# Two low parts of each mixed token set move from VectorE to GpSimd, at the three places where products of seven begin

## The reference, cut to what matters

```python
b_g, c_g, v, z = jnp.split(h @ w_in, 4, axis=-1)     # convolution layer, in
...
return y @ w_out, padded[:, -(CONV_WIDTH - 1):]       # convolution layer, out
...
return (o * jax.nn.silu(z)) @ w_out                   # attention layer, out
```

## Time and profile before

| | value |
|---|---|
| three executions, median (us) | 2051.11 |
| the profiled execution, own time (us) | 2052.14 |
| its span in the trace (us) | 2050.5 |
| TensorE busy | 1978.3 us, 96% |
| TensorE weight load busy | 1865.1 us, 91% |
| VectorE busy | 1304.5 us, 64% |
| ScalarE busy | 805.1 us, 39% |
| GpSimd busy | 237.8 us, 12% |
| mean granted TensorE clock | 0.99 |

### The profile page before, as it was taken

How to read it: one execution, slowest core, us unless ns; L and a number is a source line. 1 busy time by engine, 2 the same in 40 slices (tenths; PEclk the granted TensorE clock), 3 DMA queues, 4 the chain that set the end, 5 groups by cost and what they waited for, 6 DMA issues and landing times.

```text
span 2050.5 us, 42506 instructions
## 1 busy us (share of the span) xinstructions
PE 1978.3 (96%) x16316; PEld 1865.1 (91%) x16316; DVE 1304.5 (64%) x1992; ACT 805.1 (39%) x1222; POOL 237.8 (12%) x155
## 2 busy tenths in 40 slices
PE   4989999999999999999999999999999999999995
PEld 3889999999999999999999999999888876679995
DVE  4677777777777777797778820223443446659777
ACT  3243333333333333455455532223453434435443
POOL 1200000000000000000000333333122122201002
PEclk9999999999999999999999999999999999999997
DMA  9966655555555556744464222335313249752447
GB/s 392 406 214 220 206 202 190 190 197 205 205 206 199 198 194 207 258 142 135 140 249 175 84 83 83 103 124 170 93 52 101 82 156 340 232 162 91 141 158 268
DMA packets 128276, 371.79 MB, mean 181 GB/s; under 512 B 13170, under 2 KB 39666, under 8 KB 125874
## 3 DMA queue, kind: packets, MB, share of 16 engines
q1 hardware_dynamic: 123058, 353.64, 49.4%
q0 software_dynamic: 5120, 16.78, 2.7%
HBM read 343.76 MB, written 26.61 MB: 181 GB/s over the span
## 4 chain that ended last, share of the span: by engine, by line
PE 87%; DVE 5%; DMA 4%; ACT 1%; issue 1%; SPq 1%; POOL 0%; DVEq 0%; ACTq 0%
PE ps L879 31%; PE ps L883 15%; PE ps L767 8%; PE ps L774 4%; PE ps L833 3%; DMA s<-adastream 3%; PE ps L1335 3%; PE ps L1219 2%; PE ps L1361 2%; PE ps L1186 2%; PE ps L1201 2%; PE ps L1276 2%; PE ps L819 1%; PE ps L841 1%; PE ps L1159 1%; DMA w_raw<-wstream 1%
## 5 line engine op out<-in xcount | busy, mean ns | idle before, releaser
L715 POOL TENSOR_TENSOR w_split<-w_raw,w_split 128x1024 fp32r<-128x1024 f32 x78 | 191.8, 2459 | 1520.3 <-ACT w_split L1421 1520.3
L1483 ACT ACTIVATE w_split<-w_raw 128x1024 fp32r<-128x1024 f32 x176 | 186.3, 1058 | 332.7 <-PE ps L883 183.6
L1988 DVE TENSOR_TENSOR w_split<-w_raw,w_split 128x1024 fp32r<-128x1024 f32 x181 | 221.6, 1224 | 113.1 <-ACT w_split L1483 110.8
L879 PE MATMUL ps<-operand_hi,w_split 128*128 128x288 f32 x1056 | 283.4, 295 | 0.0
L879 PE MATMUL ps<-operand_lo,w_split 128*128 128x288 f32 x1056 | 283.3, 295 | 0.0
L879 PE MATMUL ps<-t_hi,w_split 128*128 128x288 f32 x960 | 262.9, 300 | 1.1 <-DVE c_u L2136 1.1
L879 PE MATMUL ps<-t_lo,w_split 128*128 128x288 f32 x960 | 258.0, 295 | 0.0
L879 PEld LDWEIGHTS ps<-operand_lo,w_split 128*128 128x128 f32 x1056 | 198.5, 188 | 0.0
L879 PEld LDWEIGHTS ps<-operand_hi,w_split 128*128 128x128 f32 x1056 | 198.4, 188 | 0.0
L1421 ACT ACTIVATE w_split<-w_raw 128x1024 fp32r<-128x1024 f32 (+1 forms) x90 | 93.6, 1040 | 258.3 <-PE ps L774 173.3
L879 PEld LDWEIGHTS ps<-t_hi,w_split 128*128 128x128 f32 x960 | 180.5, 188 | 10.5 <-issue 8.9
(11 more groups left out here) (375 smaller groups left out, 4076.6 us busy)
## 6 DMA issues: line engine op xcount, KB each, us to landing
w_raw<-wstream SPq DMA_DIRECT2D x183, 512.0 KB, 3.3
ada_ring<-adastream SPq DMA_DIRECT2D x114, 512.0 KB, 4.8
a<-wstream SPq DMA_DIRECT2D x88, 512.0 KB, 4.6
s<-wstream SPq DMA_DIRECT2D x44, 512.0 KB, 3.2
ada_first_ring<-adastream SPq DMA_DIRECT2D x32, 512.0 KB, 9.3
ada_third<-adastream SPq DMA_DIRECT2D x32, 512.0 KB, 6.5
x_residual<-x_in SPq DMA_DIRECT2D x8, 1152.0 KB, 8.7
tiles<-y_park SPq DMA_DIRECT2D x8, 1152.0 KB, 7.8
```

The source lines that it names most:

```text
L715: pool.tensor_tensor(WL[:, n.slot, 0:width], WR[:, n.slot, 0:width], WH[:, n.slot, 0:width].bitcast(F32), ALU.subtract).then_inc(w_lo_read ...
L879: pe.matmul(PS[:, bank, 0:HALF], WH[:, c.slot, k * P:(k + 1) * P], x(k), start=(first and k == 0 and x is hi), stop=False, skip_group_chec ...
L1483: act.activation(WH[:, c.slot, :], raw, ACT.Copy).then_inc(w_hi_ready, 1)
L1988: dve.tensor_tensor(WL[:, c.slot, :], raw, WH[:, c.slot, :].bitcast(F32), ALU.subtract).then_inc(w_lo_ready, 1)
```

## The change

The low parts of kinds 2 and 3 are made by GpSimd, by the same operation on the same 128x2304 operands, in all three places; those of kinds 0 and 1 stay with VectorE. In GpSimd's queue the four instructions of the first two places stand right behind the eight first chunks; the two of the third place stand behind the chunk `W_OUT + 3`. Each waits for the same counts of `t_hi` and `t_raw` as VectorE did. Their completion is counted by a new semaphore, `t_lo_late`, and TensorE waits for its counts 1 to 6 before products 4 and 6 of the first units; the counts of `t_lo` are renumbered. To make room for the semaphore, `h1_hi` is dropped and its 16 signals go on the existing `xg_hi`, with counts that go on from 16.

```diff
+            def mixed_lo(kind, kh, a, hi, raw):
+                pool.wait_ge(t_hi, hi)
+                pool.wait_ge(t_raw, raw)
+                pool.tensor_tensor(TL[:, HK * kh:HK * (kh + 1), a, :], part_block(X, kh, a), TH[:, kind, :, :].bitcast(F32),
+                                   ALU.subtract).then_inc(t_lo_late, 1)
+            mixed_lo(2, 0, 1, 4, 7)
+            mixed_lo(3, 1, 0, 5, 7)
+            def mixed_out(y, kind, kh, a, hi, raw):
+                pool.wait_ge(t_hi, hi)
+                pool.wait_ge(t_raw, raw)
+                pool.tensor_tensor(TL2[:, HK * kh:HK * (kh + 1), a, :], part_block(B1, kh, a), TH2[:, mixed_slot(y, kind), :, :].bitcast(F32),
+                                   ALU.subtract).then_inc(t_lo_late, 1)
+            mixed_out(0, 2, 0, 1, 8, 11)
+            mixed_out(0, 3, 1, 0, 9, 11)
             pool.wait_ge(w_lo_ready, W_MLA + 2)
...
             rest(Chunk(W_OUT + 3))
+            mixed_out(1, 2, 0, 1, 12, 15)
+            mixed_out(1, 3, 1, 0, 13, 15)
...
                 pe.wait_ge(t_hi, 4)
-                pe.wait_ge(t_lo, 5)
+                pe.wait_ge(t_lo_late, 1)
                 product(operand(m, u, 4), *T_3, b, False, False)
...
-                pe.wait_ge(t_lo, 6)
+                pe.wait_ge(t_lo_late, 2)
                 product(operand(m, u, 6), *T_4, b, False, True)
...
                 if q == 1:
-                    pe.wait_ge(t_lo, 9 + 4 * y)
+                    pe.wait_ge(t_lo_late, 3 + 2 * y)
                 product(pair_operand(y, q, 4), *U_3, b, False, False)
...
                 part_sum(RA12, RA12, RA11, ALU.subtract, (part_sums, summed(n, 2)), (w_lo_ready, operand(m, u, 3).at(1)))
-                if first:
-                    mixed_lo(2, 0, 1, 4, 7, 0, HK)
                 consume(2)
...
                 part_lo(operand(m, u, 4), RA21[:, :])
-                if first:
-                    mixed_lo(3, 1, 0, 5, 7, 0, HK)
                 consume(3)
...
-                if q == 1 and y == 0:
-                    mixed_out(0, 2, 0, 1, 8, 11)
                 part_lo(pair_operand(y, q, 3), RA12)
-                if q == 1 and y == 1:
-                    mixed_out(1, 2, 0, 1, 12, 15)
...
                 part_lo(pair_operand(y, q, 4), RA21[:, :])
-                if q == 1:
-                    mixed_out(y, 3, 1, 0, 9 + 4 * y, 11 + 4 * y)
                 pair_add(y, q - 1, 1)
```

More of the change, by code:

```diff
@@ L349, in build @@
         part_sums, part_copied, part_evac = sem("part_sums"), sem("part_copied"), sem("part_evac")
-        t_raw, t_hi, t_lo, pre_copied = (sem(n) for n in ("t_raw", "t_hi", "t_lo", "pre_copied"))
+        t_raw, t_hi, t_lo, t_lo_late, pre_copied = (sem(n) for n in ("t_raw", "t_hi", "t_lo", "t_lo_late", "pre_copied"))
         pre_done = sem("pre_done")
@@ L366, in build @@
         h1_normed, h1_prompt_done = sem("h1_normed"), sem("h1_prompt_done")
-        h1_raw, h1_hi, h1_ready = sem("h1_raw"), sem("h1_hi"), sem("h1_ready")
+        h1_raw, h1_ready = sem("h1_raw"), sem("h1_ready")
         xg_read = sem("xg_read")
@@ L1078, in pair_products @@
                 if q == 1:
-                    pe.wait_ge(t_lo, 7 + 4 * y)
+                    pe.wait_ge(t_lo, 5 + 2 * y)
                 product(pair_operand(y, q, 1), *U_1, c, True, False)
@@ L1082, in pair_products @@
                 if q == 1:
-                    pe.wait_ge(t_lo, 8 + 4 * y)
+                    pe.wait_ge(t_lo, 6 + 2 * y)
                 product(pair_operand(y, q, 2), *U_2, b, True, False)
@@ L1094, in pair_products @@
                 if q == 1:
-                    pe.wait_ge(t_lo, 10 + 4 * y)
+                    pe.wait_ge(t_lo_late, 4 + 2 * y)
                 product(pair_operand(y, q, 6), *U_4, b, False, True)
@@ L1694, in h1_high @@
                         act.wait_ge(w_used, W_MLA)
-                    act.activation(OH[:, k * T:(k + 1) * T], B1[:, k * T:(k + 1) * T], ACT.Copy).then_inc(h1_hi, 1)
+                    act.activation(OH[:, k * T:(k + 1) * T], B1[:, k * T:(k + 1) * T], ACT.Copy).then_inc(xg_hi, 1)
             round_k_rope(Chunk(W_KV + W_THREE + 2))
@@ L2413, in h1_low @@
                 for k in range(HG * q, HG * q + HG):
-                    rest(k, h1_hi, k + 1, h1_ready)
+                    rest(k, xg_hi, KT + k + 1, h1_ready)
             h1(0)
```

## The result

The changed kernel takes 2073.99 us (median of 4 runs, 2072.54 to 2074.43), the kernel before 2051.51 us beside it (4 runs, 2050.09 to 2052.14). The ratio is 1.0108, with a 95% interval of 1.0095 to 1.0121: slower by 22.5 us. The forecast was 2074.3. That it fits this closely is luck: one term was too small, two were too large, and some time was won where the forecast had none.

A forecast was written before the change was run, and what follows sets the result against it. The prediction took TensorE, nearly unbroken, as the bound, waiting on VectorE's ordered queue. Places 5.7 + 7.0 + 6.5 = 19.2 us, plus 4.0 for the clock, made 23.2 on 2051.11: 2074.3 us, range 2063 to 2083.

The forecast's parts named there:

- Exclusion: All three places: VectorE operations with two SBUF inputs stand during each GpSimd subtraction, up to 5.3 us each.
- First place: Near 138 to 152 us: product 4 is 6.8 us late, less a vanished 1.1 us wait; 5.7 us before the clock.
- Second place: Near 899 to 916 us: product 2 is 5.0 us late, low weight part 3 later; 7.0 us before the clock.
- B: GpSimd's second moved operation at each place, kind 3's low part; taken to last 5.3 us.
- The rival: Second place: GpSimd enters ahead of kind 1's low part, product 2 is 10.1 us late; chance 0.2 with a dearer clock.
- the row at 1144.89: Kernel before: GpSimd waits through four packed VectorE operations, taking 3.82 us; read as packed runs holding GpSimd off.
- Third place: Near 1869 to 1888 us: ScalarE's rounding 5.0 us late, product 4's second part delayed; 6.5 us before the clock.
- A: GpSimd's first moved operation at each place, kind 2's low part; taken to last 5.3 us.
- The clock: TensorE drops to 1.2 GHz after idle times at the three places, costing 2.5, 0.3 and 1.2, together 4.0 us.
- GpSimd at every boundary: All three places: GpSimd enters at every boundary, or the clock is dearer; 28 to 31 us lost, chance 0.2.
- The gain without exclusion: All three places: GpSimd's wide operations let VectorE through, gaining 3.7 us, 2047.4 us; chance 0.05.

The follow-up runs named there:

- runs with writes: Changed kernel with each of GpSimd's six subtractions replaced by three fills of its target, which read nothing from SBUF: 2048.07 us against 2050.94 for the kernel before.
- with pieces: Changed kernel with each GpSimd subtraction cut into four of 128x576: 2063.91 us, ratio 1.0066 to the kernel before.
- the warm run: Changed kernel with dummy matmuls (17, 50 and 25) put into TensorE's three idle times: 2070.83 us, ratio 1.0098 to the kernel before.
- B behind kind 1: Changed kernel where, at the second place, GpSimd's second operation waits until VectorE has made kind 1's low part: 2071.1 us, ratio 1.0094 to the kernel before.
- short operations: Changed kernel with VectorE's weight sum and kind 1's low part at the second place each split in four: 2073.58 us, ratio 1.0114 to the kernel before.
- the second reorder: Kernel before, nothing moved to GpSimd, VectorE's queue reordered at the three places, with sums of squares and last gate moved later too: 2048.36 us against 2051.0.

## Why the prediction came out right, step by step

**Exclusion: right.** A GpSimd row that waits for nobody takes 5.16 us (the first of the six; 5.3 was taken), the others 5.5 to 6.2 with their own wait. L2004 and L2009 are drawn out to 5.3 to 6.1 us, and the runs with writes and with pieces show that this, and its length, is the loss.

**First place: the working held.** Product 4 was to be 6.8 us late; its evacuation starts at 151.49 + 0.34 - 145.57 = 6.3 us late (0.34 us is what this execution was ahead by). The slow stage then cost 2.5 us, as forecast, and 1.4 came back where the 1.1 us wait had been. With the clock, 8.2 were forecast and 7.35 measured; in other runs with the same first place it came out at 6.2 to 7.4, with the stage at 0.50 beginning earlier or later.

**Second place: the step that failed.** The forecast read: "kind 1's low part, packed behind it, is 5.0 us late", and let B in only in the gap behind the clearing, at 910.0. B got in one boundary earlier, ahead of kind 1's low part. That part ended at 903.87 before and ends at 920.57 now; less the 7.0 us of the first place it is 9.7 late. The terms behind it changed too: product 3's wait for its low weight part was to remain and carry 7.0; it went, and with it the 0.4 us for the next evacuation (2.0 won), and the slow product 2 cost 2.2 where 0.3 was set down, as nothing behind it was late any more. So the place costs about what product 2 is late, 9.7, and 9.9 by the matmuls' starts, with 7.3 forecast. The rival had this entry, with 10.1 us for product 2. The Trainium skill's rule (page "SBUF — State Buffer", section "Who interferes with whom": the order of issue decides who blocks, and whoever issues first has the shared pair for the whole instruction) gives the same, and B's entry agrees; the row at 1144.89, by which I had set the rule aside, misled.

**Third place: the lateness held, the clock's term did not.** A drew out the first sum instead of the second, which is the same for ScalarE's rounding: 5.0 us late as forecast. Low weight part 4 ends at 1903.81 - 15.84 = 1887.97, with 1888.3 forecast (15.84 us is what had been lost by then). But the forecast took the slow stage at 2.5 us, let the wait for low weight part 4 absorb 1.3 and added 1.2. Product 2 came 4.8 us late and lost 1.9 at half speed, 0.3 came back behind it, and TensorE never waited for low weight part 4, which was there 0.7 us before its use: 6.4 us, not 7.7. The warm run shows the other side: without the slow clock the place costs 5.7, and then low weight part 4 is waited for.

**The clock: 4.0 forecast, 2 to 5 measured.** The ratios of the changed kernel and of the warm one differ by 0.0010, 2 us, less than their intervals resolve; their profiles give 4.5. The sum was near, the split was not: 2.5, 0.3 and 1.2 were forecast; the warm run gives 1.6, 2.2 and 0.7. The first is a lower end, for in that run the dummies held product 4 back by some 0.9 us, and the clock fell once, at 146.2, before they took effect; in the changed kernel itself the slow stage cost 2.5 there.

So 8.2 + 7.3 + 7.7 = 23.2 was forecast and 7.35 + 9.9 + 6.4 = 23.6 measured; a term 2.6 too small and two that were 0.9 and 1.3 too large. The other 1.3 us, won outside the places, were in no term; a stage at 0.50 that the kernel before has at 1821.5, and the changed one has not, moves the difference there by 1.6 alone. The range held for a better reason than the sum: it rested on the exclusion, and only who gets in first was open.

**The rivals' sums.** Two of them don't add up as written. "GpSimd at every boundary" was given 28 to 31 us, while 21.2 and half of 10.2 make 26.3. The gain without exclusion was given as 3.7 us, while its terms, 2.25 and 1.3, make 3.55; the fills brought 2.4.

**Left open: the row at 1144.89.** In all twelve kernels it takes 3.81 to 3.83 us for 2.39, while three packed VectorE operations of 128x576 beside it keep their 0.75. Some 78 us on GpSimd is held again, in the timeline of the kernel before:

```profile
1221.18 2.76 DVE L2472 TENSOR_TENSOR q_latent_lo<-q_latent,q_latent_hi 128x576 fp32r<-128x576 f32 x4
...
1223.01 3.19 POOL L715 TENSOR_TENSOR w_split<-w_raw,w_split 128x1024 fp32r<-128x1024 f32 x1 [6.19 <-ACT w_split L1421]
```

The four of VectorE are undisturbed, and GpSimd's takes 0.8 us too long. Part of this is a matter of asking in time, which the forecast overlooked. GpSimd asked 0.17 us ahead of the start of VectorE's next operation here, 0.13 us ahead of the first boundary at 1144.89, and at the second place of the changed kernel A asked within 0.02 us of the sum of 905.99: each time it missed that boundary. The shortest notice with which it got in was 0.21 us, in the warm run:

```profile
1880.52 5.28 POOL L735 TENSOR_TENSOR t_lo_out<-tiles,t_hi_out 128x2304 fp32r<-128x2304 f32 x1 [10.80 <-ACT t_hi_out L1593]
1880.73 6.15 DVE L2009 TENSOR_TENSOR a<-w_raw,a 128x1024 f32<-128x1024 f32 x1
```

That leaves one boundary without an account, the second at 1144.89, which came 0.80 us after asking. The row is GpSimd's first operation after 1026.69 us of idleness; no run tests whether that matters.

## What to carry to other kernels

Before moving a two-input subtraction from VectorE to GpSimd, add to its price, for each operation moved, up to GpSimd's own duration on whatever VectorE operation with two SBUF inputs comes next, and see who waits for that one; here 2.55 us of relief cost 4.5 us of standing on average (27.1 us for six). If the offload must be, cut it in pieces or place it where the next VectorE operation is one that nobody waits for (those runs won back some 9 and some 3 us of the 22.5, the latter within the error of the times). And look first at what the relief can bring: TensorE's waits at the places were 6.1 us, and with GpSimd's work made free only 2.4 came.

## What the runs showed of the hardware that was not expected

- It isn't only operations with two inputs in SBUF that stand for GpSimd. Operations with a scalar and one input do too, beside its fill and beside its subtraction. In the run with fills the one of 128x64 at 145.76 took 2.09 us, where it takes 0.24 in the changed kernel, at a time when GpSimd is idle; in the run with pieces it took 1.38. In the kernel before, one of 128x512 took 2.48 us beside GpSimd's subtraction of 115.66, and 0.55 elsewhere. The forecast's list of who excludes whom lacked these.

```profile
145.99 1.38 DVE L2077 TENSOR_SCALAR acc<-u_sample,small 128x64 f32<-128x64 f32 x1
```

```profile
116.01 2.48 DVE L1937 TENSOR_SCALAR x_residual<-x_residual,mod_scale,mod 128x512 f32<-128x512 f32 x1
```

- GpSimd's subtraction, undisturbed, takes 1.41 us for 128x576, 2.39 for 128x1024 and 5.16 for 128x2304, and its fill of 128x2304 2.03.
- TensorE's clock fell to 1.2 GHz behind each idle time of 2.9 us and more at the three places, where nothing filled it. Behind shorter ones it went either way. With the shorter holds 2.5 us brought a fall. The first of the two idle times at the first place, 2.6 to 2.7 us, brought none in the changed kernel, where the fall came behind the 4.46 after them, but brought one in the warm run and in those with B behind kind 1 and with short operations. Behind the second place's 1.9 us the clock stayed in the kernel before and fell in the second reorder. These windows are of the kernel before, then of the second reorder:

```profile
900.00:907.00 7.00, 5.11 (x39) 4.89 (x38) 6.83 (x8) 6.63 (x13) 0.00 (x0) 1.00 0.23 77
```

```profile
903.00:906.30 3.30, 3.30 (x16) 3.30 (x16) 3.30 (x2) 1.46 (x5) 0.00 (x0) 0.50 0.03 5
```

A stage at 0.50 stretched the first sixteen matmuls of a product from 2.36 to 4.2 us; what that costs hangs on which operand is late next.
